# Softmax sums applied inside the turning product: a diagonal of inverse sums in place of the identity

## The reference

```python
p = softmax(logits)          # exp(logits - max) / sum
o = einsum('bhqk,bkhd->bqhd', p, v)
```

## Time and profile before

| | |
|---|---|
| median of 3 runs | 3419.76 us (3419.38 to 3421.25) |
| profiled execution | 3418.59 us, its span 3416.8 us |
| PE busy in the span | 3349.6 us (98%) |
| DVE, ACT, Pool busy | 2071.2, 1368.7, 161.5 us |
| first stack's attention, per layer | 121.4 and 120.5 us |
| second stack's attention | 208.2 and 158.0 us |

### The profile page before, as it was taken

How to read it: one execution, slowest core, us unless ns; L and a number is a source line. 1 busy time by engine, 2 the same in 40 slices (tenths; PEclk the granted TensorE clock), 3 DMA queues, 4 the chain that set the end, 5 groups by cost and what they waited for, 6 DMA issues and landing times.

```text
span 3416.8 us, 53567 instructions
## 1 busy us (share of the span) xinstructions
PE 3349.6 (98%) x20066; PEld 2771.9 (81%) x20066; DVE 2071.2 (61%) x3301; ACT 1368.7 (40%) x2172; POOL 161.5 (5%) x39
## 2 busy tenths in 40 slices
PE   8999999999999999999999999999999999999998
PEld 6766888888877578888889777988888988888887
DVE  7876457444679745655567655664444676565546
ACT  6556333222364553322222555352332346644323
POOL 2320000000033010000000000000000000000000
PEclk9999999999999999999999999999999999999999
DMA  4235332222222543332221001111111210123222
GB/s 146 87 142 206 111 123 103 95 98 98 87 99 99 188 159 123 111 119 99 99 97 64 26 26 46 62 62 64 70 65 62 73 63 26 58 75 110 88 98 86
DMA packets 45783, 317.14 MB, mean 93 GB/s; under 512 B 5008, under 2 KB 7312, under 8 KB 8464
## 3 DMA queue, kind: packets, MB, share of 16 engines
q1 hardware_dynamic: 44720, 307.07, 25.0%
q10 hardware_dynamic: 864, 7.31, 0.5%
HBM read 312.26 MB, written 2.10 MB: 92 GB/s over the span
## 4 chain that ended last, share of the span: by engine, by line
PE 85%; DVE 8%; ACT 2%; issue 2%; DVEq 1%; DMA 0%; POOL 0%; ACTq 0%; SPq 0%; POOLq 0%
PE psum L848 23%; PE psum L849 23%; PE psum L854 23%; PE psum L1518 3%; PE psum L1555 2%; PE psum L1539 2%; DVE MA L2603 1%; PE psum L934 1%; PE psum L997 1%; DVE S L2552 1%; PE psum L1481 1%; PE psum L956 1%; DVE xn L2447 1%; PE psum L1483 1%; DVE top L2583 1%
## 5 line engine op out<-in xcount | busy, mean ns | idle before, releaser
L848 PE MATMUL psum<-xh,whi 128*128 128x512 f32 (+1 forms) x2224 | 853.8, 386 | 3.8 <-issue 1.6
L849 PE MATMUL psum<-xl,whi 128*128 128x512 f32 (+1 forms) x2224 | 847.6, 383 | 0.0
L1757 ACT ACTIVATE whi<-wst 128x2048 fp32r<-128x2048 f32 x229 | 437.5, 1910 | 540.0 <-PE psum L854 527.5
L2349 DVE TENSOR_TENSOR wlo<-wst,whi 128x2048 fp32r<-128x2048 f32 x197 | 451.3, 2291 | 165.2 <-ACT whi L1757 163.0
L854 PE MATMUL psum<-xh,wlo 128*128 128x512 f32 (+1 forms) x2224 | 536.3, 383 | 0.1
L848 PEld LDWEIGHTS psum<-xh,whi 128*128 128x128 f32 x2224 | 418.0, 188 | 95.7 <-issue 14.5
L849 PEld LDWEIGHTS psum<-xl,whi 128*128 128x128 f32 x2224 | 418.1, 188 | 81.2 <-issue 1.0
L854 PEld LDWEIGHTS psum<-xh,wlo 128*128 128x128 f32 x2224 | 409.9, 188 | 82.2 <-POOL wlo L813 0.5
L813 POOL TENSOR_TENSOR wlo<-wst,whi 128x2048 fp32r<-128x2048 f32 x34 | 160.7, 4728 | 1083.1 <-ACT whi L1757 1082.8
L848 PE MATMUL psum<-uh,whi 128*128 128x512 f32 x480 | 186.9, 389 | 0.0
L849 PE MATMUL psum<-ul,whi 128*128 128x512 f32 x480 | 186.7, 389 | 0.0
(11 more groups left out here) (419 smaller groups left out, 5864.2 us busy)
## 6 DMA issues: line engine op xcount, KB each, us to landing
wst<-weights SPq DMA_DIRECT2D x287, 1024.0 KB, 4.8
dft<-c_dft ACTq DMA_DIRECT2D x2, 2688.0 KB, 9.0
hT<-x_t SPq DMA_DIRECT2D x4, 512.0 KB, 9.1
wst<-weights SPq DMA_DIRECT2D x2, 512.0 KB, 6.7
cT<-ctx_t ACTq DMA_DIRECT2D x1, 1024.0 KB, 6.8
out<-hT SPq DMA_DIRECT2D x1, 1024.0 KB, 4.9
out<-hT SPq DMA_DIRECT2D x2, 512.0 KB, 3.7
masks<-c_masks SPq DMA_DIRECT2D x1, 644.0 KB, 12.4
```

The costliest lines, as they stand in the source:

```text
L848: pe.matmul(out, weights(m.whi, k), head(k), start=opens and n == 0, stop=False)
L849: pe.matmul(out, weights(m.whi, k), tail(k), start=False, stop=False)
L1757: act.activation(m.whi[:, slot, :], m.wst[:, slot, :], ACT.Copy).then_inc(s.hi_ready, 1)
L2349: TT(m.wlo[:, slot, :], m.wst[:, slot, :], m.whi[:, slot, :].bitcast(F32), ALU.subtract).then_inc(s.lo_ready, 1)
```

## The change

The identity in `turn` becomes a diagonal matrix with the inverse sums of the head on its diagonal, and the transpose becomes a product of the same operands: block as stationary, diagonal as moving. So PT holds finished probabilities. `denominators` goes on TensorE and on ScalarE, as do `Rs`, its two pairs of semaphores, and the multiplication in `normalized`, which is now a copy. What is new is the diagonal: an elementwise product of the identity and the inverse sums, 128 x 256, in two buffers. In the first stack Pool makes it for units 0 to 32 of each layer, before the last two tails, and VectorE for units 33 to 35; in the second stack VectorE makes it for every unit. `reciprocals` moves to the head of VectorE's turn, ahead of the next unit's maxima; in the first stack `normalized` moves behind the maxima, and ScalarE takes both exponentials of the next unit before the copies of this one.

```diff
+POOL_UNITS = FIRST_A + 9
@@ pool
+            def diagonals(l, u):
+                if u >= 2:
+                    pool.wait_ge(s.t_done, l * RING1 + RING["T", u - 2, chunks_of(u - 2) - 1] + 1)
+                elif l:
+                    pool.wait_ge(s.t_done, l * RING1)
+                pool.wait_ge(s.rden_ready, l * N_UNITS + u + 1)
+                rden = m.rden[:, 2 * (u % 4):2 * (u % 4) + 2]
+                nc.gpsimd.tensor_tensor(m.diag[u % 2][:, :, :], ident.unsqueeze(1).broadcast_to([P, 2, P]),
+                                        rden.unsqueeze(2).broadcast_to([P, 2, P]), ALU.mult).then_inc(s.diag_pool, 1)
...
+                for u in range(POOL_UNITS):
+                    diagonals(l, u)
+                for c in (SL_MERGE, SL_MERGE + 1):
+                    split(l * SLABS1 + c)
@@ turn, first stack
-                pe.wait_ge(s.exp_ready, 2 * (l * N_UNITS + u + 1))
+                if u < POOL_UNITS:
+                    pe.wait_ge(s.diag_pool, l * POOL_UNITS + u + 1)
+                else:
+                    pe.wait_ge(s.diag_dve, (l + 1) * (N_UNITS - POOL_UNITS) + u - N_UNITS + 1)
...
-                    last = pe.transpose(ps[bank][:, (b % 4) * P:(b % 4 + 1) * P],
-                                        scores(u, b % 2)[:, (b // 2) * P:(b // 2 + 1) * P], ident)
+                    last = pe.matmul(ps[bank][:, (b % 4) * P:(b % 4 + 1) * P],
+                                     scores(u, b % 2)[:, (b // 2) * P:(b // 2 + 1) * P], m.diag[u % 2][:, b % 2, :],
+                                     start=True, stop=True)
@@ turn, second stack
-                    pe.wait_ge(s.exp2_ready, 2 * (unit0 + u + 1))
+                    pe.wait_ge(s.diag2_ready, unit0 + u + 1)
...
-                        last = pe.transpose(...)
+                        last = pe.matmul(..., m.S2[...], m.diag2[u % 2][:, b % 2, :], start=True, stop=True)
@@ both stacks: denominators() and its calls go, on TensorE and on ScalarE
-                    last = pe.matmul(ps[6][HD * par:HD * (par + 1), P:2 * P], m.rden[:, c:c + 1].broadcast_to([P, HD]),
-                                     ident, start=True, stop=True)
...
-                act.activation(m.Rs[:, u % 2, :], ps[6][:, P:2 * P], ACT.Copy).then_inc(s.rs_copied, 1)
@@ normalized, both stacks
-                dve.wait_ge(s.rs_copied, l * N_UNITS + u + 1)
...
-                TT(into, ps[6][:, 0:P], m.Rs[:, u % 2, :], ALU.mult).then_inc(s.o_ready, 1)
+                nc.vector.tensor_copy(into, ps[6][:, 0:P]).then_inc(s.o_ready, 1)
@@ VectorE's turn, first stack
+                    reciprocals(l, u)
+                    if u and u + 1 < N_UNITS:
+                        maxima(l, u + 1)
                     if u >= 2:
                         normalized(l, u - 2)
-                    if u and u + 1 < N_UNITS:
-                        maxima(l, u + 1)
-                    reciprocals(l, u)
@@ reciprocals, second stack (called first in VectorE's turn now, ahead of maximum(u + 1, 0))
-                    nc.vector.reciprocal(m.rden2[:, c:c + 2], m.den2[:, c:c + 2]).then_inc(s.rden2_ready, 1)
+                    nc.vector.reciprocal(m.rden2[:, c:c + 2], m.den2[:, c:c + 2])
+                    dve.drain()
+                    if u >= 2:
+                        dve.wait_ge(s.t2_done, RING2["T", l, u - 2, blocks2(l, u - 2) // 4 - 1] + 1)
+                    TT(m.diag2[u % 2][:, :, :], ident.unsqueeze(1).broadcast_to([P, 2, P]),
+                       m.rden2[:, c:c + 2].unsqueeze(2).broadcast_to([P, 2, P]), ALU.mult).then_inc(s.diag2_ready, 1)
```

More of the change, by code:

```diff
@@ L509, in two_stacks @@
         m.rows, at = place(nc, at, "rows", [P, 256])
-        m.Rs, at = place(nc, at, "Rs", [P, 2, P])
+        diag0, at = place(nc, at, "diag0", [P, 2, P])
         m.den, at = place(nc, at, "den", [P, 8])
@@ L516, in two_stacks @@
         m.warm, at = place(nc, at, "warm", [P, 1])
+        diag1, at = place(nc, at, "diag1", [P, 2, P])
+        m.diag = diag0, diag1
         assert at <= 229376, at
@@ L572, in two_stacks @@
         m.PT2, at = place(nc, at, "PT2", [P, 5, 4 * P])
-        m.Rs2, at = place(nc, at, "Rs2", [P, 2, P])
+        diag2_0, at = place(nc, at, "diag2_0", [P, 2, P])
         m.none, at = place(nc, at, "none", [P, 1])
@@ L606, in two_stacks @@
         m.Ko = ko0, ko1
+        diag2_1, _ = place(nc, ko0_area + 4 * TA, "diag2_1", [P, 2, P])
+        m.diag2 = diag2_0, diag2_1
         m.Koh = [place(nc, area, f"koh{i}", [P, TA], F32R)[0] for i, area in enumerate((ko0_area, ko1_area))]
@@ L1538, in turn @@
                         kb = 2 * c + b // 2
-                        last = pe.transpose(ps[bank][:, b * P:(b + 1) * P],
-                                            m.S2[:, 2 * (u % 2) + b % 2, kb * P:(kb + 1) * P], ident)
+                        last = pe.matmul(ps[bank][:, b * P:(b + 1) * P],
+                                         m.S2[:, 2 * (u % 2) + b % 2, kb * P:(kb + 1) * P], m.diag2[u % 2][:, b % 2, :],
+                                         start=True, stop=True)
                     last.then_inc(s.t2_done, 1)
@@ L1559, in weighted @@
                             mm.then_inc(s.pv2_done, 1)
[L1561 to L1568, removed]
                 for n in range(4):
@@ L1947, in _ @@
                 for u in range(N_UNITS + 1):
-                    for par in range(2):
-                        if u and u + 1 < N_UNITS:
[L1950 to L1955, removed]
+                    for par in range(2 if u and u + 1 < N_UNITS else 0):
+                        exponential(l, u + 1, par)
+                    if u < N_UNITS:
+                        copies(l, u, range(chunks_of(u)))
                     modulation(l, u)
@@ L2181, in exponential @@
                     if unit >= 4:
-                        act.wait_ge(s.rden2_ready, unit - 3)
+                        act.wait_ge(s.diag2_ready, unit - 3)
                     act.wait_ge(s.max2_ready, 2 * unit + par + 1)
@@ L2194, in copy @@
                     act.activation(m.PT2[:, chunk % 5, :], ps[4 + at % 2][:, :], ACT.Copy).then_inc(s.t2_act, 1)
[L2196 to L2202, removed]
                 def spectra(numbers):
@@ L3134, in _ @@
                     here = {place_: project_at(l, p + 1, n, place_) for place_ in ("mid", "end")}
+                    if u < len(units):
+                        reciprocals(u)
                     if u + 1 < len(units):
```

37 lines of the change are left out of this document (12 added, 25 removed).

## The result

The changed kernel takes 3533.73 us (median of 4 runs, 3533.42 to 3537.5) against 3419.57 us of the kernel before beside it: ratio 1.0336, 95% interval 1.0318 to 1.0354. It is slower by 114 us; the forecast was 3511 us, 91 us slower.

A forecast was written before the change was run, and what follows sets the result against it. TensorE, busy for 3349.6 of 3416.8 us, was taken as the bound: 3418.6 + 113.2 (products) - 30.4 (denominators) - 20 (old waits) + 24 + 4 (diagonal waits) = 3509.4, so 3511 us; range 3468 to 3558.

The forecast's parts named there:

- Products and old waits: TensorE's turns: second records for 984 blocks add 113.2 us; 20 of 25 us of idle time in attention go.
- The growth of a unit: Each unit grows by 0.22 to 0.7 us on TensorE, so VectorE and ScalarE have more time.
- Denominators: TensorE: 132 units each lose four records, 0.23 us a unit, saving 30.4 us.
- The waits for the diagonal: TensorE's turns wait for the diagonal: 24 us in the second stack, 4 us in the first.
- The rival in which VectorE's chain bounds the second stack: Second stack: VectorE's chain becomes the bound; 0.9 us a unit gives 3541 us, 1.3 us gives 3565; chance 0.15.
- First stack: Waits for the diagonal there: 0.06 us a unit, 4 us for 72 units; bounds 0 and 14 us.
- my own bound of 5: The prediction is wrong if the time outside attention moves by more than 5 us, since nothing there is touched.
- The signs: Expected in the profile: 1248 and 720 turn records, loads of about 190 ns, four blocks in some 1.1 us, longer stretches.
- The product as cheap as the transpose: TensorE's turns: a product costs 0.109 us a block like the transpose, total 3398 us; chance 0.05.
- the fourfold product: TensorE's turns: a product costs four transposes, 321.8 us in place of 113.2, total 3720 us; chance 0.02.

The follow-up runs named there:

- The kernel with transposes: Changed kernel with transposes back in the turns, the diagonals built and waited for but not used: 3437.49 us, ratio 1.0054 to the kernel before.
- the product kernel: Kernel before with products with the identity in place of its 984 transposes, all else kept: 3506.27 us, ratio 1.0257.
- the kernel with Pool's block and one product: Kernel before, inverses written to a 128-column block, mostly by Pool, turned by one product in place of two: 3431.55 us, ratio 1.0040.

## Why the prediction was right, and its terms

**Products and old waits: right.** +113.2 - 20 = 93 was forecast, 88.2 measured alone. The page of that kernel has 107.1 us more busy and 20.1 us less idle time; with the products at 113 the old waits were 25. The growth of a unit was understated, at 0.22 to 0.7 us: a latent unit has 12 blocks and grows by 12 x 0.115 - 0.23 = 1.15.

**Denominators: right.** -30.4 forecast; -29 where the products are in place. (In the reading of the earlier trace rows it is the fourth record that starts 0.12 us after the first; the next work starts 0.32 after the first and 0.20 after the fourth, as the sum has it.)

**The waits for the diagonal: the mechanism right, the size half.** 24 + 4 = 28 us forecast, 55 measured. In the second stack 40.5 us, 0.68 a unit, where I took 0.4. The three units of the earlier trace rows had given 0.5; I lowered it, since longer turns would give VectorE room. The kernel with transposes shows that in the second stack they give none: its waits there are the same. VectorE stands idle for 78.3 us in all ahead of `OT`, which starts at the end of TensorE's `weighted`, just before the next turn, however long the turn was, and the works behind it push the inverse back. The sample also held no unit like that at 2002.19, 2.12 us late. The rival in which VectorE's chain bounds the second stack, with 0.9 us a unit to 3541, named the place rightly; the truth lies between it and the forecast.

**First stack.** 4 us forecast, about 14 there: 1.8 + 5.5 in the stretches and some 7 ahead of them. I weighed Pool's diagonal against VectorE's selection in the earlier trace rows and passed over unit 0, whose inverse stands behind a rotation that waits for ScalarE. That the time outside the stretches moved by 5.3 us, just past my own bound of 5, comes from this. I also wrote that nothing changes by Pool's last two tails. But VectorE makes the last diagonals beside them, and these took up to 3.3 us in place of 0.43 (last section); TensorE's named waits for them are only 1.2 us.

**The sum.** Forecast 3511, measured 3534. The waits for the diagonal were 27 us too small in it, and the other terms together 4 us too high. That the measured time lies inside the range, and at the very top of the forecast's own 3490 to 3535, is owed to the width of the range, not to the term for the diagonal.

The signs: 1248 and 720 records, loads of 192 ns and four blocks in 1.05 us came as said. The stretches were forecast at 130, 130, 247 and 194 us and are 130.7, 134.8, 261.7 and 190.4. The waits by name for VectorE's diagonal, 32.3 us, lie inside the 15 to 35 that I gave, while their true cost does not: what the name shows is only the idle part.

**The rivals.** The product as cheap as the transpose is refuted by the product kernel; the fourfold product likewise, since 88 us measured leave no room for 322. The Trainium skill (TensorE: Matmul & The Clock Gate, section Terms) gives the factor four that the fourfold product rests on; the records here say two: one at 0.109 us against two at 0.112.

## What to carry over

Where an engine is full, count its records before and after a trade, and then ask of each new operand of it who makes it and what stands ahead of that maker in its queue: here 35 of 55 us of waits were one place in VectorE's order. A busy share hides pauses, so take the cost of waits from a kernel with the same records and no wait, not from the idle time by name. And a saved record saves only what the next work's start shows, which here hung on the shapes of the stationary operands on both sides of it.

## What the runs showed of the hardware

- After the long pauses of this kernel TensorE's clock fell, from 2.4 GHz to its lower level of 1.2 for most of the windows shown. These windows of the changed kernel lie behind the waits of 4.21 and 2.12 us (granted clock third from the end, a mean over the 4 us shown); behind the wait of 1.16 us at 2024.77 it stayed at 1.00 (2024 to 2028):

```profile
1136.00:1140.00 4.00, 1.62 (x6) 1.40 (x8) 1.71 (x6) 0.49 (x3) 1.19 (x2) 0.53 0.00 0
1140.00:1144.00 4.00, 4.00 (x30) 2.05 (x30) 2.44 (x12) 1.29 (x6) 0.61 (x1) 0.62 0.79 256
2002.00:2006.00 4.00, 3.81 (x20) 3.63 (x21) 1.60 (x6) 0.65 (x3) 0.00 (x0) 0.65 0.00 0
```

- Going from a stationary of 64 columns to one of 128 costs TensorE some 0.1 us: the next record starts 0.20 us after the last `weighted` record, where one of 64 columns starts after 0.11 (and the unit's end above). The weight load shows the step too. In the unit of the earlier trace rows the first load of 128 columns starts 0.17 us after the loads of 64 columns have ended, and together with its product, where the loads before and behind it overlap:

```profile
1993.04 0.25 PEld L1566 LDWEIGHTS psum<-cst,rden 128*64 128x64 f32 x4
1993.46 0.19 PEld L1481 LDWEIGHTS psum<-cqh,whi 128*128 128x128 f32 x1 [0.17 <-issue]
```

  The Trainium skill (TensorEngine Tiling (Array Packing), section Tiling Modes) says that changing the tiling mode drains the engine. The trace agrees as far as the load no longer runs ahead; a full drain it does not show, since the next record starts 0.20 us after one that is given 0.28. The four records of the denominators stay in the mode of `weighted`, which fits that half as many of full width saved nothing.
- VectorE's small operations beside Pool's subtractions of 4.7 us take far longer: 426 ns became up to 3309 for the diagonal, 226 up to 4376 for the copy. In the kernel with Pool's block and one product two subtractions last from 337.19 to 346.41; VectorE's copy that starts at 343.87 ends at 346.49, just behind them. In the changed kernel (ns: least, median, longest):

```profile
L2548 DVE TENSOR_TENSOR diag<-cst,sm x6: 426/1980/3309, 341.4 to 1269.2; 128x256 f32<-128x256 f32 x6
```
